# Third and fourth group of pooled sums on GpSimd held until the narrow unit's scans are done; scores and first sigmoid of the second unit ahead of the turned rows

## What is computed

```python
for g, w in enumerate(POOL_WINDOWS):              # 2, 4, 8, 16
    win_sum = cs[:, POOL_HIST + 1:...] - cs[:, POOL_HIST + 1 - w:...]
    d = win_sum / count[None, :, None] - ext[:, POOL_HIST:, sl]
    outs.append(jnp.einsum('btc,ce->bte', d, w_pool[g]))

z = jnp.einsum('bqhd,bkhd->bhqk', q, k) * (HEAD_DIM ** -0.5) + sb_bias
log_keep = jnp.where(visible, jax.nn.log_sigmoid(-z), 0.0)
later = lax.cumsum(log_keep, axis=3, reverse=True) - log_keep
a = jnp.where(visible, jnp.exp(jax.nn.log_sigmoid(z) + later), 0.0)
out = jnp.einsum('bhqk,bkhd->bqhd', a, v)
```

## Time and profile before

| | us |
|---|---|
| median of 3 runs | 1124.99 |
| lowest, highest | 1124.26, 1125.95 |
| the profiled execution | 1124.56 |
| its span, first to last instruction | 1122.8 |
| PE busy in the span | 1092.2 |
| DVE, ACT, POOL busy | 446.7, 330.9, 170.9 |

### The profile page before, as it was taken

The page is one execution under the profiler, slowest core; times in us unless marked ns, Lnnn a source line. Parts: engine busy times, 40 slices in busy tenths (PEclk is TensorE's granted clock), DMA queues, the critical chain, the costliest instruction groups (busy, mean ns, idle before and its releaser), DMA issues.

```text
span 1122.8 us, 26890 instructions
## 1 busy us (share of the span) xinstructions
PE 1092.2 (97%) x11636; PEld 796.2 (71%) x11636; DVE 446.7 (40%) x833; ACT 330.9 (29%) x648; POOL 170.9 (15%) x149
## 2 busy tenths in 40 slices
PE   8999999999999999999899999999999999999995
PEld 7999999966665559999766666666666666666663
DVE  6326654378875543345822212212212222122121
ACT  6323332266775552223211111111111111111111
POOL 0001200599200000000001111111111111111111
PEclk9999999999999999999999999999999999999998
DMA  7356684000126368464699999999999999999991
GB/s 240 112 154 208 213 268 138 1 13 2 39 69 195 115 224 292 152 251 175 266 342 403 382 389 384 394 378 386 392 373 388 386 385 387 391 392 387 385 352 34
DMA packets 85696, 293.05 MB, mean 261 GB/s; under 512 B 13376, under 2 KB 44800, under 8 KB 59958
## 3 DMA queue, kind: packets, MB, share of 16 engines
q1 hardware_dynamic: 78405, 273.69, 64.9%
q0 software_dynamic: 7168, 17.58, 6.7%
HBM read 272.98 MB, written 42.87 MB: 281 GB/s over the span
## 4 chain that ended last, share of the span: by engine, by line
PE 90%; DVE 4%; DMA 3%; ACT 1%; issue 1%; POOL 0%; SPq 0%; ACTq 0%; POOLq 0%; DVEq 0%
PE bank L2093 14%; PE bank L2515 11%; PE bank L2519 10%; PE bank L2523 9%; PE bank L2325 8%; PE bank L2549 5%; PE bank L2553 5%; PE bank L2557 4%; PE bank L2136 4%; PE bank L2302 3%; PE bank L2265 3%; PE bank L2494 2%; PE bank L2174 2%; DMA wo_raw<-in_w_out 2%; PE bank L2535 1%
## 5 line engine op out<-in xcount | busy, mean ns | idle before, releaser
L2515 PE MATMUL bank<-w_ring,xeT 128*32 128x256 f32 x1536 | 342.6, 380 | 0.0
L2519 PE MATMUL bank<-w_ring,xeT 128*32 128x512 f32 x1536 | 265.7, 594 | 0.7 <-ACT xeT L1502 0.7
L2515 PEld LDWEIGHTS bank<-w_ring,xeT 128*32 128x32 f32 x1536 | 166.2, 110 | 54.2
L2549 PE MATMUL bank<-w_ring,hT 128*32 128x256 f32 x768 | 171.7, 380 | 0.0
L1975 DVE SCALAR_TENSOR_TENSOR hid<-sgl,gtab,bank 96x256 f32<-96x256 f32 x32 | 21.9, 683 | 338.0 <-ACT sgl L1508 338.0
L2523 PE MATMUL bank<-w_ring,xeT 128*32 128x256 f32 x1536 | 155.8, 379 | 0.0
L2553 PE MATMUL bank<-w_ring,hT 128*32 128x512 f32 x768 | 133.2, 595 | 1.6 <-ACT hT L1514 1.6
L2093 PE MATMUL bank<-w_hi,xh 128*128 128x256 f32 (+1 forms) x432 | 124.6, 288 | 2.5 <-DVE xl L1575 2.5
L2093 PE MATMUL bank<-w_hi,xl 128*128 128x256 f32 (+1 forms) x432 | 121.6, 281 | 0.0
L2093 PE MATMUL bank<-w_lo,xh 128*128 128x256 f32 (+1 forms) x432 | 121.6, 281 | 0.0
L1711 DVE TENSOR_TENSOR_SCAN keep<-keep,unseen 128x1024 f32<-128x1024 f32 (+7 forms) x64 | 94.6, 1511 | 38.0 <-ACT keep L1287 37.8
(11 more groups left out here) (277 smaller groups left out, 1641.7 us busy)
## 6 DMA issues: line engine op xcount, KB each, us to landing
w_ring<-in_w_gate SPq DMA_DIRECT2D x64, 1024.0 KB
w_ring<-in_w_up SPq DMA_DIRECT2D x64, 1024.0 KB
w_ring<-in_w_down SPq DMA_DIRECT2D x64, 1024.0 KB
k_scr<-in_cache_k SPq DMA_DIRECT2D x32, 256.0 KB, 3.4
v_scr<-in_cache_v SPq DMA_DIRECT2D x32, 256.0 KB, 3.4
pgk<-k_scr SPq DMA_DIRECT2D x32, 256.0 KB, 4.1
w_raw<-in_w_in SPq DMA_DIRECT2D x7, 1024.0 KB, 6.3
pgv<-v_scr SPq DMA_DIRECT2D x4, 1024.0 KB, 7.1
```

The costliest lines, as they stand in the source:

```text
L2515: return pe.matmul(up_right_ps(i, g), xeT[i][:, k, rows_of(g)], w[1][:, k, FA:F], start=first and g != 1, stop=ends, skip_group_check=True)
L2519: pe.matmul(gate_ps(i)[rows_of(g), :], xeT[i][:, k, rows_of(g)], w[0][:, k, :], start=first, stop=ends, skip_group_check=True)
L2549: return pe.matmul(y_right_ps(g), hT[:, ft, rows_of(g)], w[:, ft, DA:D], start=first and g != 1, stop=ends, skip_group_check=True)
```

## The change

Two edits. POOL waits, before `diff(2)`, until `s_p` has reached 2 * 4 + 2 = 10, which is after both scans of the narrow unit. And the scores of unit 1 on PE, and its first sigmoid on ACT, are issued before the last turned rows and no longer behind them; the second sigmoid of unit 1 stays where it was.

```diff
@@ POOL
             for g in range(NG):
+                if g == 2:
+                    pool.wait_ge(s_p, 2 * TAIL + 2)
                 diff(g)
@@ ACT, behind the copies of u
                 if i == NUS - 2:
                     for a in range(2):
                         keep_head(0, a)
+            keep_head(1, 0)
             act.wait_ge(s_ut, NG)
             act.activation(up_rows[:, :], bank[0:TAILP, 6, :], ACT.Copy).then_inc(s_ur, 1)
             act.activation(us_rows[:, :], bank[0:TS, 7, :], ACT.Copy).then_inc(s_ur, 1)
@@ ACT, loop over units
-                if 0 < i < NU:
+                if 1 < i < NU:
                     keep_head(i, 0)
@@ PE
             scores(0)
             project_u(NUS - 1)
+            scores(1)
             transpose_u(NG - 1)
 
             for i in range(NU + 2):
-                if 0 < i < NU:
+                if 1 < i < NU:
                     scores(i)
```

## The result

The changed kernel takes 1131.78 us (median of 5 runs, 1130.36 to 1132.25), the kernel before on the same chip 1124.38 (5 runs, 1124.26 to 1125.95). The ratio is 1.0054 with an interval of 1.0044 to 1.0065: slower, by some 6 us on the ratio (the two medians lie 7.4 apart), where the forecast was 1125.8 with a range up to 1128.4. The profiled run took 1131.98 us, its span is 1130.1 (before: 1124.56 and 1122.8).

The account below looks back on a forecast made before the run. PE bounds the kernel (90% of the chain), other engines counting only where PE waits; -2.3 us at the front plus 3.1 at unit 11 gave +0.8 on the 1124.99 median: 1125.8 us, range 1122.6 to 1128.4.

Parts of the forecast that it names:

- The front: Start of the attention, units 1 to 6: shorter scans and waits bring scores 6 2.3 us sooner.
- the edit alone therefore gives 0.2: Unit 1: issuing its scores and first sigmoid earlier brings scores 2 from 240.03 to 239.8, 0.2 us.
- POOL's later work: POOL's sums after the hold: group 3 starts about 260.4 and ends at 283.6, group 4 ends at 310.
- the second rival: Unit 11: POOL also holds the eight query-spreading copies; 2.1 us on top, +2.9 in all, 1127.9 us; chance 0.28.
- A scan and a POOL instruction never run together: Rule for DVE and POOL: whichever is second waits for the other's end; with both queued they alternate.
- Units 5 to 9 without harm: Units 5 to 9: POOL's later work costs PE nothing, as DVE ran beside POOL there before too.
- The string at unit 11: DVE's work from 295.87 us meets POOL's group 4; PE's next sum 5.3 us after scores 11, not 2.2: loss 3.1.
- nothing in this trace shows an instruction of that kind held: Argument against POOL holding the eight one-input spread copies at unit 11, the rival given chance 0.28.
- All cases: After unit 11: in the forecast, what follows hangs on PE and carries the shift on unchanged.
- the loss bound of 6.8: Unit 11: upper bound if each of four scans meets a full POOL addition, 6.8 us (1129.5); left out of the range.

Follow-up runs that it names:

- hold_only: Changed kernel with POOL's wait alone, scores and first sigmoid of unit 1 put back where they were: 1131.57 us, ratio 1.0056 against the kernel before.
- early_only: Changed kernel without POOL's wait, keeping the earlier scores and first sigmoid of unit 1: 1124.52 us, ratio 0.9993 against the kernel before.
- after_again: The changed kernel run once more, unaltered, on one chip with filled_again: 1131.93 us, ratio 1.0052 against the kernel before.
- filled_wait: Changed kernel plus 22 PE transposes of the identity, product unread, ahead of unit 11's wait for DVE: 1127.53 us, ratio 1.0013 against the kernel before.
- filled_again: filled_wait run once more, on one chip with after_again: 1127.85 us, ratio 1.0023 against the kernel before.
- spread_on_act: Changed kernel with the eight query-spreading copies issued by ACT instead of DVE, ahead of unit 10's sigmoids: 1123.62 us, ratio 0.9985 against the kernel before.

## Why the prediction was wrong

- **The front, -2.3 us by scores 6: right in sum, wrong in its parts.** The lead is 2.29 at that place. Scores 2 at 239.77 (forecast 239.8), L1711 0.17 (under 0.2), scans 2.26 to 2.32 (the very first, which touches POOL, 2.42), POOL from 260.39 (260.4). But the working gave 2.1 to POOL's wait, which hold_only bears out (2.0), and 0.2 to the early scores, where early_only shows 1.8. That the sum came out at 2.3 all the same is luck: the two gains overlap. The step "the edit alone therefore gives 0.2" followed PE and ACT to scores 2 and stopped there; it didn't ask on which of POOL's instructions DVE's would then fall.
- **POOL's later work: right.** Group 3 ended at 283.61 (283.6). Group 4 ended at 307.47, forecast 310. The 2.5 us are the second rival's: POOL goes on in the pauses of the copies.
- **"A scan and a POOL instruction never run together": wrong, by before's own trace.** POOL's and DVE's timelines of before:

```profile
279.02 2.83 POOL L1086 TENSOR_SCALAR wsum<-wsum 128x1025 f32<-128x1025 f32 x1
```

```profile
279.30 4.56 DVE L1711 TENSOR_TENSOR_SCAN keep<-keep,unseen 128x896 f32<-128x896 f32 x2 [1.64 <-ACT keep L1287]
```

Two scans of 896 columns take some 4.0 us when nothing holds them (single ones 1.99 and 2.00). Held until the `TENSOR_SCALAR` ended at 281.86, the two would have ended near 285.8; they ended at 283.86. The rule of the prediction holds for POOL's additions, not for this instruction.
- **Units 5 to 9 without harm: right.** The lead of 2.29 stood unchanged from 265 to 298 us.
- **The string at unit 11, +3.1 us: this step failed.** It counted the four scans of units 9 and 10 as held, and the eight copies as free. The scans of unit 9 were held (5.09 us for two), those of unit 10 weren't (3.41), and the copies were: 4.0 us more. The step from scores to sum grew by 5.1 us, not by 3.1. The argument that was weighed too high was "nothing in this trace shows an instruction of that kind held". The trace had no such copy beside POOL at all, so it spoke for neither side.
- **The page of the Trainium skill was right on the copies.** The Trainium skill, SBUF — State Buffer, "Who interferes with whom", lets a copy take the pair of ports that DVE shares with GpSimd. The traces agree that such copies are held (1.62 against 5.66 and 5.72 us), though they show no ports; and the second rival, which was that rule worked out on this kernel, gives the mechanism and the place, and its price to a tenth: a shift of +2.9 at unit 11 was worked out, and +2.83 measured. It had 0.28 of the chance, against 0.49 for the forecast, though the trace spoke for neither and the page for it.
- **The half clock behind the wait: in no case of the prediction.** All cases carried the shift at unit 11 on to the end unchanged. With a wait of 3.5 to 6 us on the engine that bounds the kernel, the clock belonged in the sum. It makes 1127.9 of the second rival into about 1130.3, by the 2.4 us that the stretch cost. The trace of before has a place that should have raised the question, a wait of 3.18 us in the router's stage with half clock behind it, though not a clean one: two other profiles have the same fall there behind a wait of 0.63 us. PE's timeline and a stretch of before:

```profile
554.59 0.41 PE L2428 MATMUL bank<-eb,before 48*128 48x32 f32 x2 [3.18 <-DVE eb L1837]
```

```profile
557.00:560.00 3.00, 3.00 (x13) 2.75 (x14) 1.20 (x4) 0.00 (x0) 0.92 (x1) 0.50 0.00 0
```

After, hold_only and after_again, the three with a wait of 5.8 us there, have the fall within half a microsecond of 304.5; no other kernel has one there, filled_wait and filled_again among them, which have the same late DVE.
- **The last 2 us of the spans** are not all the change's. Nine of the thirteen profiles have a short stretch at half clock between 507 and 553 us, kernels without a long wait among them; before's has none. The one in after's router stage costs 1.6 of the 7.3 us between the spans. That it comes from the change is not shown.
- **The range** ended at 1128.4, since the loss bound of 6.8 was left out and the second rival's own price had no room above it. The loss bound alone, 1129.5, would not have reached 1131.8 without the clock.

## What to carry to other kernels

Work that is held back doesn't vanish: list what it will stand beside, and treat each DVE instruction there that moves SBUF to SBUF as held by a busy GpSimd until a trace of such a meeting shows it free, small copies as well. A trace in which two things never met says nothing about their meeting. And where PE is the bound, price a wait of several microseconds at more than its length: look at the granted clock behind it, and look in the trace at hand for a wait of that length. Here moving four matmuls and a sigmoid brought most of what the wait on POOL brought, without moving POOL's work: try the parts of a change alone.

## What the runs showed of the hardware

- POOL's `TENSOR_SCALAR` of 1025 columns ran from 299.92 to 302.75 in after, and DVE's scan, begun at 301.02, was not held by it: two scans in 3.41 us. The last copy, begun at 299.99, took 1.00, and early_only's maximum at 255.47 was free under another `TENSOR_SCALAR`. In before, the first of the two scans begun at 279.30 ended at 281.94, 2.64 us instead of 2.0. So in these places POOL let DVE go about 1 us into an instruction of 2.83 us; its additions held DVE to their end.
- In an idle stretch of 5.8 us on PE at 2.4 GHz the clock fell to half before the stretch was over, in three profiles of three (after, hold_only, after_again), from about 304.5 to 311 us. Waits of up to 1.23 us at that place were followed by full clock. All thirteen profiles, before's too, have one more stretch at half clock in the router's stage, between 546 and 571 us; in eight of them it comes behind a wait of 3.2 us, in three behind one of 1.6 and in two (early_only, hold_only) behind one of 0.63.
- A shorter wait can do it too, but not each time. All seven profiles of kernels with both parts of the change have a wait of 1.52 us near 238 us. In three of them (after_again, filled_again, spread_on_act) half clock follows from 239.7 on and costs 1.6 to 1.7 us; in the other four, after among them, the clock stays at 1.00. None of the six profiles with a smaller wait there has the fall. PE's timeline of after_again, ahead of it, and the clock of the stretch behind:

```profile
238.03 1.22 PE L2268 MATMUL bank<-ident,keep 128*128 128x128 f32 x8 [1.52 <-ACT qsum L1398]
```

```profile
240.00:243.00 3.00, 3.00 (x8) 0.70 (x5) 1.86 (x1) 0.68 (x2) 0.00 (x0) 0.50 0.07 22
```

Seven against six are too few to call this shown.
- The clock also fell, for a shorter stretch, while PE was busy without a gap (540 to 545 us in after: busy 5.00 of 5.00, clock 0.68). What brings this on is open.
